# Two RMS norms of a second transformer block applied behind their projections instead of ahead of them, and the spread of a rate row moved behind the third query tile

## The chip, the cores and the metric

The kernel runs on one core of a Trainium2 chip. TensorE (PE) multiplies matrices into PSUM, VectorE (DVE) and ScalarE (ACT) work element by element, GpSimd (POOL) does one elementwise job here and issues a few DMAs, and SyncE (SP) issues nearly all DMAs. The metric is the time of one execution in microseconds (us); lower is better.

## The reference, cut to what matters

Two blocks run one after the other on a sequence of 512 tokens of width 1024, all in fp32. The first ends with a mixture of experts and a norm; the second begins with a norm of that norm's result, and has another norm ahead of its feed-forward part:

```
# end of the first block
h2 = rmsnorm(x, norm2_w[l])
x = x + expert_choice_ffn(h2, w_router[l], w_gate[l], w_up[l], w_down[l])
...
return rmsnorm(x, norm_f_w)
# second block
h = rms_norm(x, pre_mix_g[l])
proj = h @ w_in[l]          # q, k, v; a recurrent branch; two gates
...
merged = gate_a * (y_a @ proj_a[l]) + gate_b * (y_b @ proj_b[l])
x = x + rms_norm(merged @ w_out[l], post_mix_g[l])
hf = rms_norm(x, pre_ffn_g[l])
u = jnp.square(jax.nn.relu(hf @ w_up[l])) @ w_down[l]
x = x + rms_norm(u, post_ffn_g[l])
```

A norm multiplies each token's row by one number, its rate (one over the root of the mean square), and each column by a weight. The rate of a token is a factor of every product of that token's row with a matrix, so it can be applied to the product as well.

## The kernel before, in words

All work is written out by hand, a queue of instructions per engine, with semaphores between them. The activations lie as `X`, tokens on partitions in 4 tiles (`tc`) of 128, and as `HT`, features on partitions in 8 tiles (`dc`) of 128 by 512 tokens.

Projections take fp32 numbers apart into a high and a low part: ScalarE copies a 1 MB block of weights in rounded form (`split2_act`), GpSimd subtracts that from the block (`splits2_pool`, one instruction per block), and TensorE does three products for each of the 8 `dc` (`split_tile`), 24 matmuls for one tile of 128 output features. Two tiles use one block of weights. Activations are taken apart likewise: ScalarE writes the rounded `HT` (`norm_out_act`), VectorE writes the rest (`norm_low_dve`), for the second block in `LOW3` and `LOW4`. Weight blocks rotate through three slots and two buffers for the high part, so a block is split when the block two before it has been used.

A norm before a projection was done like this. ScalarE squares and sums the rows of `X`, takes a logarithm and an exponential, each of another table, and has the rates `rs`. VectorE makes four diagonal matrices of them (`norm_dve`). TensorE multiplies `X` by the diagonals, which transposes and scales at once (`norm_pe`, 32 matmuls). ScalarE and VectorE then write the high and low parts, and the first projection tile follows them `dc` by `dc`. While TensorE waits for the rates it multiplies something that nobody uses (`keep_busy`).

Where the blocks meet: the last scatter of the experts adds 8 results in PSUM to `ACCX` on VectorE, and each finished row tile is multiplied there by the weight of the first block's last norm, `NORMF`, into `X`. ScalarE squares both (`final1_act`), so that one rate for both norms comes out. The load of the first weight block for the second block (`("qk", 0)`) starts when the last scatter is done.

ScalarE copied the query and key tiles (`band_act`), the 14 tiles of the recurrent branch (`shift_act`) and the relu of the 32 feed-forward tiles (`ffn_act`) out of PSUM, and took the tanh of the gates from PSUM directly (`merge2_act`). Two PSUM banks took turns. GpSimd waited for `n4_dg`, the diagonals of the second norm, before it split the first feed-forward block `("u", 0)`.

The opening of the first block already had its rate behind the projections: `rates_pe` multiplies a matrix of ones by the diagonals, which gives a tile with each token's rate in every row, and `rates_dve` multiplies the cosine and sine tables by it. It stood behind the second query tile, and each tile's rotation (`rotate`) behind the following one.

## Time and profile before

| | |
|---|---|
| median of 3 runs | 2925.87 us (2925.63 to 2927.24) |
| profiled execution | 2916.92 us, span 2915.1 us |
| mean granted TensorE clock | 0.969 of full |
| TensorE busy | 2641.9 us, 91% |
| VectorE busy | 940.4 us, 32% |
| ScalarE busy | 747.0 us, 26% |
| GpSimd busy | 590.8 us, 20% |

The profile is of one execution, and that one was about 9 us shorter than the median of the runs. Differences are therefore worked out inside the profile. TensorE's row says which engine carries the span; where it stands idle, the bracket at the end of its row names how long and what ended the idle time. The end of a pipelined matmul is modelled, so starts are read rather than ends. The places that matter here are three: about 26 us (the opening), 1895 to 1970 us (between the blocks) and 2527 to 2560 us (ahead of the feed-forward part).

### The profile page before, as it was taken

To read this page: it belongs to the slowest core of one execution; us is meant where nothing else is said; L and a number is where in the kernel's file an instruction comes from. 1 tells how busy PE (TensorE), PEld (TensorE's weight loads), DVE (VectorE), ACT (ScalarE), POOL (GpSimd) and SP (SyncE) were. 2 spreads that over 40 slices of the span, in tenths; PEclk is the share of its full clock that TensorE was granted. 3 is DMA by queue.
4 is the path that set the end of the run, shared out by engine and by line. 5 is a ranking of instruction groups with operands and counts; after the bars stand their busy time and mean duration, and the time that the engine had idled before them with its cause. 6 is when DMAs were issued, how large, how long until landed. Compare 5 with 4: busy or idle time off the path is not lost.

```text
span 2915.1 us, 34223 instructions
## 1 busy us (share of the span) xinstructions
PE 2641.9 (91%) x14415; PEld 1726.3 (59%) x14415; DVE 940.4 (32%) x1655; ACT 747.0 (26%) x1258; POOL 590.8 (20%) x181
## 2 busy tenths in 40 slices
PE   8999979889999998898889988898968899999998
PEld 6766767676658542332333323365757766888886
DVE  3267766753212301101011011034474521240221
ACT  3257634532112010010000100054341222422222
POOL 3301645622122000000000000031301022244442
PEclk9999979989999999999999999999988999999999
DMA  4302203113225799999999999942200033322231
GB/s 160 116 16 77 69 30 116 58 40 121 87 84 219 299 428 428 428 428 429 429 428 428 429 429 428 383 134 84 66 1 16 2 120 103 109 94 101 87 102 72
DMA packets 131045, 559.37 MB, mean 192 GB/s; under 512 B 7320, under 2 KB 88672, under 8 KB 103272
## 3 DMA queue, kind: packets, MB, share of 16 engines
q1 hardware_dynamic: 130056, 551.28, 48.0%
q0 software_dynamic: 864, 6.29, 0.6%
q8 instruction: 95, 1.56, 0.2%
q14 instruction: 30, 0.25, 0.0%
HBM read 547.01 MB, written 10.54 MB: 191 GB/s over the span
## 4 chain that ended last, share of the span: by engine, by line
PE 70%; DMA 13%; DVE 9%; ACT 5%; issue 2%; POOL 0%; DVEq 0%; SPq 0%; ACTq 0%; POOLq 0%
DMA S<-in_w_up 11%; PE PS L611 8%; PE PS L613 8%; PE PS L612 8%; PE PS L2211 7%; PE PS L2178 7%; PE PS L601 4%; PE PS L2161 2%; PE PS L3327 2%; PE PS L3330 2%; PE PS L3329 2%; PE PS L3174 2%; PE PS L2222 1%; DMA S<-in_w_down 1%; PE PS L597 1%
## 5 line engine op out<-in xcount | busy, mean ns | idle before, releaser
L2473 POOL TENSOR_TENSOR r_block<-S,r_block 128x2048 fp32r<-128x2048 f32 x57 | 261.5, 4588 | 1484.8 <-ACT r_block L2462 1476.0
L2178 PE MATMUL PS<-S 128*64 128x512 f32 x2048 | 457.1, 596 | 72.9 <-DMA S<-in_w_up 68.7
L611 PE MATMUL PS<-r_block,r_block 128*128 128x512 f32 x1040 | 417.8, 402 | 4.2 <-POOL r_block L2473 2.0
L613 PE MATMUL PS<-r_block,r_block 128*128 128x512 f32 x1040 | 405.3, 390 | 0.0
L612 PE MATMUL PS<-r_block,r_block 128*128 128x512 f32 x1040 | 404.8, 389 | 0.0
L2178 PEld LDWEIGHTS PS<-S 128*64 128x64 f32 x2048 | 141.0, 137 | 379.8 <-issue 247.4
L491 POOL TENSOR_TENSOR r_block<-S,r_block 128x2048 fp32r<-128x2048 f32 x40 | 183.4, 4586 | 550.4 <-ACT r_block L483 330.1
L2211 PE MATMUL PS<-S 128*64 128x512 f32 x1024 | 225.6, 597 | 6.3 <-DMA S<-in_w_down 3.1
L611 PEld LDWEIGHTS PS<-r_block,r_block 128*128 128x128 f32 x1040 | 195.3, 188 | 50.6 <-issue 9.2
L612 PEld LDWEIGHTS PS<-r_block,r_block 128*128 128x128 f32 x1040 | 195.4, 188 | 45.2 <-issue 6.0
L613 PEld LDWEIGHTS PS<-r_block,r_block 128*128 128x128 f32 x1040 | 195.2, 188 | 41.4
L2345 DVE SCALAR_TENSOR_TENSOR S<-S,PS 128x512 f32<-128x512 f32 x32 | 22.0, 687 | 486.9 <-ACT S L2273 463.5
L2211 PEld LDWEIGHTS PS<-S 128*64 128x64 f32 x1024 | 75.8, 138 | 145.1 <-issue 140.4
L2462 ACT ACTIVATE r_block<-S 128x2048 fp32r<-128x2048 f32 x57 | 108.9, 1912 | 172.2 <-PE PS L3330 117.6
L601 PE MATMUL PS<-S 128*128 128x512 f32 x256 | 110.5, 592 | 0.0
L2352 DVE TENSOR_TENSOR S<-S,PS 128x512 f32<-128x512 f32 x32 | 20.6, 684 | 257.2 <-PE PS L2178 257.2
L483 ACT ACTIVATE r_block<-S 128x2048 fp32r<-128x2048 f32 x40 | 76.4, 1909 | 99.6 <-DMA S<-in_w_in 68.8
L3327 PE MATMUL PS<-r_block,r_block 128*128 128x512 f32 x256 | 99.8, 390 | 1.4 <-ACT S L3346 1.4
L3329 PE MATMUL PS<-r_block,r_block 128*128 128x512 f32 x256 | 99.6, 389 | 0.0
L3330 PE MATMUL PS<-r_block,r_block 128*128 128x512 f32 x256 | 99.6, 389 | 0.0
L3369 DVE TENSOR_TENSOR S<-S 128x512 f32<-128x512 f32 x32 | 37.9, 1185 | 188.7 <-ACT S L3346 188.7
L601 PEld LDWEIGHTS PS<-S 128*128 128x128 f32 x256 | 48.6, 190 | 59.6 <-issue 59.3
(478 smaller groups left out, 3702.4 us busy)
## 6 DMA issues: line engine op xcount, KB each, us to landing
S<-in_w_gate SPq DMA_DIRECT2D x64, 2048.0 KB, 18.0
S<-in_w_up SPq DMA_DIRECT2D x64, 2048.0 KB, 21.0
S<-in_w_down SPq DMA_DIRECT2D x64, 2048.0 KB, 25.6
S<-in_w_in SPq DMA_DIRECT2D x57, 1024.0 KB, 5.4
S<-in_w_up SPq DMA_DIRECT2D x16, 1024.0 KB, 5.4
S<-in_w_down SPq DMA_DIRECT2D x16, 1024.0 KB, 4.8
S<-decay_rows SPq DMA_DIRECT2D x8, 1024.0 KB, 6.9
S<-in_w_out SPq DMA_DIRECT2D x8, 1024.0 KB, 5.0
```

Of the source, the lines that this page charges most:

```text
L491: pool.tensor_tensor(r32(w), w, rounded(WH[k % 2]), ALU.subtract).then_inc(sem("w_low"), 1)
L601: mm = pe.matmul(out, w[:, dc, off:off + P], src[:, dc, :], start=(dc == 0), stop=(dc == DC - 1))
L611: pe.matmul(out, wh, r32(HT[:, dc, :]), start=(dc == 0), stop=False)
L612: pe.matmul(out, wh, r32(low[:, dc, :]), start=False, stop=False)
L613: mm = pe.matmul(out, wl, r32(HT[:, dc, :]), start=False, stop=(dc == DC - 1))
L2178: mm = pe.matmul(PS[c * CAP:(c + 1) * CAP, 2 + 2 * m + g, :], XE[:, 2 * q + r, e * CAP:(e + 1) * CAP], w[:, r, 1024 * g + 512 * c:1024 * g ...
L2211: mm = pe.matmul(PS[c * CAP:(c + 1) * CAP, 6 + half, :], HE[e][:, f, :], w[:, f % 4, 512 * half:512 * half + 512], start=(f == 0), stop=(f ...
L2462: act.activation(r32(WH[k % 2]), slot2(name), ACT.Copy).then_inc(sem("w2_high"), 1)
L2473: pool.tensor_tensor(r32(w), w, rounded(WH[k % 2]), ALU.subtract).then_inc(sem("w2_low"), 1)
L3327: pe.matmul(PS[:, n, :], uh, r32(grid(wh.rearrange("p a b -> p (a b)"), 2)[:, f % 2, s]), start=first, stop=False)
L3329: pe.matmul(PS[:, n, :], uh, r32(wl[:, f % 2, s]), start=False, stop=False)
L3330: mm = pe.matmul(PS[:, n, :], ul, r32(grid(wh.rearrange("p a b -> p (a b)"), 2)[:, f % 2, s]), start=False, stop=last)
```

## The change

The opening uses four banks (0, 1, 5, 6) and four buffers for the raw query and key tiles, rates stand behind the third tile, and rotations one tile later. In the second block both norms are applied behind their projections. Unscaled `X` is transposed as its row tiles get ready, the high and low parts are made at once, and the rates are worked out while the first three tiles run. A tile `RSB` with the rates in every row is then spread (`spread_rates_pe` behind the third tile, `spread_rates_dve`), and VectorE multiplies each projection by it on its way out of PSUM. The weight of the first block's last norm goes into `pre_mix` for the projections, and into `X` by `block1_rows_dve`.

```diff
@@ attention_pe, opening
-                split_tile(pe, PS[:, p % 2, :], parts_of(("qk", p // 2)), P * (p % 2), HTL, "n1_lo" if p == 0 else None)\
-                    .then_inc(sem("qk_proj"), 1)
-                if p == 1:
-                    rates_pe(pe)
-                if p:
+                split_tile(pe, PS[:, QK_BANK[p % 4], :], parts_of(("qk", p // 2)), P * (p % 2), HTL, "n1_lo" if p == 0 else None)\
+                    .then_inc(sem("qk_proj"), 1)
+                if p == 2:
+                    rates_pe(pe)
+                    rotate(0)
+                if p >= 2:
                     rotate(p - 1)
@@ experts_pe, new: the last scatter, with the transposes between
+            def last_scatter():
+                pe.wait_ge(*count("mo_y", 4 * PAIRS))
+                for m in range(8):
+                    if m >= 2:
+                        pe.wait_ge(*count("mo_acc", 8 * (PAIRS - 1) + m - 1))
+                    pe.matmul(PS[:, 6 + m % 2, :], (SELT, SELT2)[m % 2][:, (m // 2) * P:(m // 2 + 1) * P],
+                              YE[:, 512 * (m % 2):512 * (m % 2) + 512], start=True, stop=True)\
+                        .then_inc(sem("mo_scattered"), 1)
+                    if m % 2 and m >= 3:
+                        first_turns(m // 2 - 1)
+                first_turns(TC - 1)
+                pe.wait_ge(*count("mo_acc", 8 * PAIRS))
+                for dc in (6, 7):
+                    for tc in range(TC):
+                        mm = pe.transpose(PS[:, dc, block_of(tc)], X[:, tc, block_of(dc)], ident)
+                    mm.then_inc(sem("n3_tp"), 1)
@@ experts_dve
-                dve.tensor_tensor(x, x, PS[:, m % 2, :], ALU.add).then_inc(sem("mo_acc"), 1)
-                if m % 2:
-                    dve.wait_ge(*count("mo_acc", 8 * (PAIRS - 1) + m + 1))
-                    dve.tensor_tensor(X[:, m // 2, :], ACCX[:, m // 2, :], NORMF, ALU.mult).then_inc(sem("x2_done"), 1)
+                dve.tensor_tensor(X[:, m // 2, s], ACCX[:, m // 2, s], PS[:, 6 + m % 2, :], ALU.add).then_inc(sem("mo_acc"), 1)
+                if m in (3, 5):
+                    weighted_rows_dve(dve, m // 2 - 1)
@@ new
+        def weighted_rows_dve(dve, tc):
+            dve.wait_ge(*count("mo_acc", 8 * (PAIRS - 1) + 2 * (tc + 1)))
+            if tc >= 2:
+                dve.wait_ge(*count("n3_sq", tc))
+            dve.tensor_tensor(XW[tc], X[:, tc, :], NORMF, ALU.mult).then_inc(sem("n3_w"), 1)
+        def block1_rows_dve(dve):
+            dve.wait_ge(*count("f1_r", 1))
+            for tc in range(TC):
+                dve.scalar_tensor_tensor(X[:, tc, :], X[:, tc, :], rs1[:, tc:tc + 1], NORMF, ALU.mult, ALU.mult)\
+                    .then_inc(sem("x2_done"), 1)
+        def spread_rates_pe(pe, tag, low):
+            pe.wait_ge(*count(tag + "_dg", TC))
+            pe.wait_ge(*count(low, DC))
+            for tc in range(TC):
+                mm = pe.matmul(PS[:, 4, block_of(tc)], ones, diag[:, tc, :], start=True, stop=True)
+            mm.then_inc(sem(tag + "_rates"), 1)
@@ splits2_pool
-                    if name == ("u", 0):
-                        pool.wait_ge(*count("n4_dg", TC))
@@ query and key tiles of the second block, now on VectorE
-                act.activation(dst, PS[:, p % 2, :], ACT.Copy).then_inc(sem("b_qk_done"), 1)
+                dve.tensor_tensor(dst, PS[:, p % 4, :], RSB, ALU.mult).then_inc(sem("b_qk_done"), 1)
@@ recurrent branch, now on VectorE
-                act.activation(PADR[:, t % 2, 1:1 + T], PS[:, t % 2, :], ACT.Copy).then_inc(sem("r_copied"), 1)
+                dve.tensor_tensor(pad[:, 1:1 + T], PS[:, t % 2, :], RSB, ALU.mult).then_inc(sem("r_copied"), 1)
@@ gates
-                        act.activation(MG_T[:, 2 * (m - 2) + j, :], PS[:, 2 * m + j, :], ACT.Tanh, scale=0.5,
-                                       bias=s_gbh[:, g:g + 1]).then_inc(sem("m2_tanh"), 1)
+                        act.activation(gate, gate, ACT.Tanh, scale=0.5, bias=s_gbh[:, g:g + 1]).then_inc(sem("m2_tanh"), 1)
+                        dve.tensor_tensor(MG_T[:, 2 * m + j, :], PS[:, 4 + 2 * m + j, :], RSB, ALU.mult).then_inc(sem("m2_scaled"), 1)
@@ ffn_pe
-            keep_busy(pe, 0, 20)
-            pe.wait_ge(*count("pn1_x", TC))
-            norm_pe(pe, "n4")
+            keep_busy(pe, 0, 12)
+            pe.wait_ge(*count("o2_copied", 8))
+            for tc in range(TC):
+                pe.wait_ge(*count("pn1_x", tc + 1))
+                for dc in range(DC):
+                    mm = pe.transpose(PS[:, dc, block_of(tc)], X[:, tc, block_of(dc)], ident)
...
-                    if t == FH * hf and hf:
-                        pe.wait_ge(*count("dn_part", 2))
-                    if t >= 2:
-                        pe.wait_ge(*count("up_relu", t - 1))
+                    if hf and t < FH + 4:
+                        pe.wait_ge(*count("dn_part", t - FH + 1))
+                    if t >= 4:
+                        pe.wait_ge(*count("up_relu", t - 3))
@@ feed-forward relu, now on VectorE
-                    act.activation(RL[:, t % 2, :], PS[:, t % 2, :], ACT.Relu).then_inc(sem("up_relu"), 1)
+                dve.scalar_tensor_tensor(r, PS[:, t % 4, :], 0.0, RSB, ALU.max, ALU.mult).then_inc(sem("up_relu"), 1)
@@ block2_pe and block2_sp
-            pe.wait_ge(*count("x2_done", TC))
-            keep_busy(pe, 7, 10)
-            norm_pe(pe, "n3")
-                if n == 0:
-                    sp.wait_ge(*count(last_scatter[0], last_scatter[1]))
```

First place: TensorE from the last expert down projection to the first projection tile of the second block. L2222 is the last scatter, L597 `keep_busy`, L589 `norm_pe`, L611 to L613 `split_tile`. Before:

```order
L2211 MATMUL PS<-S 64x512 x32
L2222 MATMUL PS<-S 128x512 x8
L597 MATMUL PS<-S 128x256 x10
L589 MATMUL PS<-S 128x128 x32
L611 MATMUL PS<-r_block_584,r_block_582 128x512
L612 MATMUL PS<-r_block_398,r_block_582 128x512
```

Of the change (L2215 is the down projection, L2235 the last scatter, L2251 `first_turns`, L2245 the transposes of the last two feature tiles):

```order
L2215 MATMUL PS<-S 64x512 x32
L2235 MATMUL PS<-S 128x512 x4
L2251 MATMUL PS<-S 128x128 x6
L2235 MATMUL PS<-S 128x512 x2
L2251 MATMUL PS<-S 128x128 x6
L2235 MATMUL PS<-S 128x512 x2
L2251 MATMUL PS<-S 128x128 x12
L2245 MATMUL PS<-S 128x128 x8
L611 MATMUL PS<-r_block_583,r_block_581 128x512
```

The 10 unused products and the 32 scaling ones are gone, and 32 transposes stand in and behind the scatter.

Second place: ScalarE over the same stretch. L2385 and L2387 are squares, L2462 is `split2_act`, L566 `norm_out_act`, L2389 to L2395 the logarithms and exponentials. Before:

```order
L2385 ACTIVATE S<-S 128x1024
L2387 ACTIVATE S<-S 128x1024
L2389 ACTIVATE S<-S 128x4
L2391 ACTIVATE S<-S 128x4
L2393 ACT_TABLE_LOAD
L2393 ACTIVATE S<-S 128x4
L2395 ACTIVATE S<-S 128x4
L2462 ACTIVATE r_block_582<-S 128x2048
L566 ACTIVATE r_block_584<-PS,S 128x512 x4
L566 ACTIVATE r_block_601<-PS,S 128x512 x4
L2401 ACTIVATE S<-S 128x1024 x4
L2462 ACTIVATE r_block_651<-S 128x2048
```

Of the change (L2418 and L2423 are the squares, L2524 the split, from the first square on):

```order
L2418 ACTIVATE S<-S 128x1024
L2524 ACTIVATE r_block_581<-S 128x2048
L2423 ACTIVATE S<-S 128x1024
L2418 ACTIVATE S<-S 128x1024
L2423 ACTIVATE S<-S 128x1024
L566 ACTIVATE r_block_583<-PS,S 128x512 x4
L566 ACTIVATE r_block_600<-PS,S 128x512 x4
L2524 ACTIVATE r_block_641<-S 128x2048
L2418 ACTIVATE S<-S 128x1024
L2423 ACTIVATE S<-S 128x1024
L2418 ACTIVATE S<-S 128x1024
L2423 ACTIVATE S<-S 128x1024
```

The first split stands behind one square instead of all eight, the high parts behind four, and the rates come last.

Third place: ScalarE ahead of the feed-forward part, from the exponential of the norm behind the mixing part (L3280) on. L507 to L519 are `norm_act`, L3346 the relu. Before:

```order
L3280 ACT_TABLE_LOAD
L3280 ACTIVATE S<-S 128x4
L507 ACT_TABLE_LOAD
L507 ACTIVATE S<-S 128x1
L514 ACTIVATE S<-S 128x1024 x4
L517 ACTIVATE S<-S 128x4
L519 ACT_TABLE_LOAD
L519 ACTIVATE S<-S 128x4
L2462 ACTIVATE r_block_651<-S 128x2048
L566 ACTIVATE r_block_584<-PS,S 128x512 x4
L566 ACTIVATE r_block_601<-PS,S 128x512 x4
L2462 ACTIVATE r_block_582<-S 128x2048
```

Of the change (L3349 is that exponential, L2524 the split):

```order
L3349 ACT_TABLE_LOAD
L3349 ACTIVATE S<-S 128x4
L2524 ACTIVATE r_block_641<-S 128x2048
L566 ACTIVATE r_block_583<-PS,S 128x512 x4
L566 ACTIVATE r_block_600<-PS,S 128x512 x4
L2524 ACTIVATE r_block_581<-S 128x2048
L3417 ACT_TABLE_LOAD
L3417 ACTIVATE S<-S 128x1
```

Squares and rates now stand behind the high parts and behind the second split.

## Rows read from the trace of the kernel before

**Rows 1.** The page's first part: busy time of the engines.

```profile
PE 2641.9 (91%) x14415; PEld 1726.3 (59%) x14415; DVE 940.4 (32%) x1655; ACT 747.0 (26%) x1258; POOL 590.8 (20%) x181
```

**Rows 2.** TensorE between the blocks: start, duration, line, tile, count, idle before and releaser.

```profile
1895.91 3.96 PE L2222 MATMUL PS<-S 128*128 128x512 f32 x8 [1.39 <-ACT S L2288]
...
1907.26 4.58 PE L597 MATMUL PS<-S 128*128 128x256 f32 x20 [2.33 <-DVE S L2373]
1911.68 7.31 PE L589 MATMUL PS<-S 128*128 128x128 f32 x64
1918.74 0.47 PE L611 MATMUL PS<-r_block,r_block 128*128 128x512 f32 x1
...
1930.39 0.50 PE L611 MATMUL PS<-r_block,r_block 128*128 128x512 f32 x1 [0.50 <-POOL r_block L2473]
```

**Rows 3.** VectorE between the blocks, same view.

```profile
1898.62 1.23 DVE L2373 TENSOR_TENSOR S<-S 128x1024 f32<-128x1024 f32 x1
...
1904.67 1.28 DVE L2370 TENSOR_TENSOR S<-S,PS 128x512 f32<-128x512 f32 x2
...
1913.49 7.01 DVE L577 SCALAR_TENSOR_TENSOR r_block<-PS,S,r_block 128x512 fp32r<-128x512 f32 x8 [2.08 <-ACT r_block L566]
```

**Rows 4.** ScalarE between the blocks, same view.

```profile
1898.62 1.06 ACT L2385 ACTIVATE S<-S 128x1024 f32<-128x1024 f32 x1 [1.34 <-DVE S L2370]
...
1910.55 1.91 ACT L2462 ACTIVATE r_block<-S 128x2048 fp32r<-128x2048 f32 x1
```

**Rows 5.** DMA issues between the blocks (KB each, us to landing), and SP's queue.

```profile
S<-in_w_in SPq DMA_DIRECT2D x13, 1024.0 KB, 5.4
...
1905.02 1.02 SPq L3487 DMA_DIRECT2D S<-in_w_in  x2
```

**Rows 6.** TensorE and ScalarE in the opening.

```profile
7.86 5.90 PE L545 MATMUL PS<-S 128*128 128x128 f32 x32 [7.86 <-DMA S<-in_x]
26.67 1.16 PE L553 MATMUL PS<-S 128*128 128x128 f32 x8 [0.75 <-DVE S L571]
...
13.10 4.73 ACT L566 ACTIVATE r_block<-PS,S 128x512 fp32r<-128x512 f32 x8 [4.92 <-PE PS L545]
```

**Rows 7.** TensorE, ScalarE and VectorE ahead of the feed-forward part.

```profile
2527.66 8.79 PE L597 MATMUL PS<-S 128*128 128x256 f32 x40
2540.48 9.01 PE L589 MATMUL PS<-S 128*128 128x128 f32 x64 [4.03 <-DVE S L571]
2549.25 0.47 PE L611 MATMUL PS<-r_block,r_block 128*128 128x512 f32 x1
...
2531.28 0.21 ACT L3280 ACTIVATE S<-S 128x4 f32<-128x4 f32 x1
...
2531.52 4.87 DVE L3286 SCALAR_TENSOR_TENSOR S<-S 128x1024 f32<-128x1024 f32 x4 [0.63 <-ACT S L3280]
```

**Rows 8.** VectorE and GpSimd where GpSimd splits a block of weights.

```profile
2065.57 0.75 DVE L2760 SCALAR_TENSOR_TENSOR S<-S 128x512 f32<-128x512 f32 x1
2066.24 5.11 DVE L2758 TENSOR_TENSOR S<-S 128x512 f32<-128x512 f32 x1
...
2066.09 4.71 POOL L2473 TENSOR_TENSOR r_block<-S,r_block 128x2048 fp32r<-128x2048 f32 x1 [1.10 <-ACT r_block L2462]
...
668.90 2.35 DVE L1736 SCALAR_TENSOR_TENSOR S<-S 128x512 f32<-128x512 f32 x1
...
666.10 4.61 POOL L491 TENSOR_TENSOR r_block<-S,r_block 128x2048 fp32r<-128x2048 f32 x1 [7.98 <-ACT r_block L483]
```

**Rows 9.** Busy time by window: PEclk is the third value from the end.

```profile
2542.00:2544.00 2.00, 2.00 (x12) 2.00 (x11) 0.86 (x2) 1.02 (x2) 2.00 (x1) 0.50 0.05 12
```

**Rows 10.** The feed-forward part: a relu, a square, and TensorE's start of the second half.

```profile
2571.33 0.60 ACT L3346 ACTIVATE S<-PS 128x512 f32<-128x512 f32 x1 [4.84 <-PE PS L613]
...
2566.52 1.56 DVE L3369 TENSOR_TENSOR S<-S 128x512 f32<-128x512 f32 x1 [3.56 <-ACT S L3346]
...
2725.82 0.47 PE L611 MATMUL PS<-r_block,r_block 128*128 128x512 f32 x1 [1.22 <-issue]
```

More of the change, by code:

```diff
@@ L642, in build_program @@
         A0 = M_DYN + 20480
-        qk_raw = at(A0, 2, T)
+        qk_raw = [at(A0 + o, T) for o in (0, 512, 2048, 2560)]
+        QK_BANK = (0, 1, 5, 6)
         qk_tmp = at(A0 + 1024, 2, T)
@@ L669, in rotate @@
                     pe.wait_ge(*count("qk_sin", p - 1))
-                pe.matmul(PS[:, 2 + p % 2, :], const("rot"), qk_raw[:, p % 2, :], start=True, stop=True)\
+                pe.matmul(PS[:, 2 + p % 2, :], const("rot"), qk_raw[p % 4], start=True, stop=True)\
                     .then_inc(sem("qk_rot"), 1)
@@ L2256, in experts_pe @@
             pe.wait_ge(*count("mo_he", 4 * PAIRS))
-            scatter(PAIRS - 1)
+            last_scatter()
         def experts_act(act):
@@ L2388, in final1_act @@
+            act.activation(warm, eps, ACT.Ln).then_inc(sem("f1_ln"), 1)
+            squares(0)
+            squares(1)
+            act.wait_ge(*count("both_norms", 1))
+            norm_out_act(act, "n3", "pre_mix")
+            split2_act(act, ("qk", 1))
+            squares(2)
+            squares(3)
             act.wait_ge(*count("f1_sq", TC))
```

146 lines of the change are left out of this document (90 added, 56 removed), and 2 rows, old and new, of the table CHAINS.

## The prediction

> **What bounds the kernel.** I read the busy times first: TensorE is busy 91% of the span and no other engine over 32% [rows 1], so time is won where TensorE stands idle or does work that nobody uses. The expert stage in the middle is paced by its weight stream and is not edited. Then I read TensorE's timeline at the three edited places. Between the blocks the last scatter runs from 1895.91 to about 1904.9, unused products fill from 1907.26, the scaling products run from 1911.68, and the first projection tile starts at 1918.74 [rows 2]. That is 13.8 us without a projection. Ahead of the feed-forward part the unused products start at 2527.66, the scaling ones at 2540.48 after 4.03 us idle, and the first tile at 2549.25: 21.6 us [rows 7]. In the opening TensorE waits 0.75 us for the diagonals [rows 6].
>
> **The opening.** Behind the third tile the diagonals are long there, so the 0.75 us go. The rate and rotation products stay the same in number. Four banks and buffers remove waits that the timeline does not show as stalls; I take nothing for them. Saved: 0.75 us.
>
> **Between the blocks.** A scatter product takes 3.96 / 4 = 0.99 us [rows 2], an addition on VectorE 1.28 / 2 = 0.64 and a multiplication of 1024 columns 1.23 [rows 3], a transpose 5.90 / 32 = 0.18 at most [rows 6]. TensorE now does 4 scatters (to 1899.9), 6 transposes, 2 scatters, 6 transposes, 2 scatters, 6 transposes, and is at about 1906.6. VectorE adds the fourth result by 1900.7, weights row tile 0 by 1902.0, adds the sixth result by 1903.7 and then comes to weighting row tile 1.
>
> Here a lock matters. While GpSimd splits a block (4.6 us), VectorE instructions with two inputs in SBUF stand still: one square of 512 columns took 5.11 us, from 2066.24 to 2071.35, where the split ran from 2066.09 to 2070.80, and the three-operand kind took 2.35 us for 0.75 beside a split that ended at 670.71 [rows 8]. VectorE had been working without a gap there, and GpSimd, which was ready at 2066.09, still came in at VectorE's next instruction. When will GpSimd split here? The load of the first block no longer waits for the last scatter, so it is issued at 1894.6 instead of 1905.02 and lands after 5.4 us [rows 5], at 1900.0. ScalarE finishes its first square of 1.06 us plus the reading of its sum at 1899.8 and splits until 1902.0, in 1.91 us [rows 4]. GpSimd then holds the lock from 1902.1 to 1906.7. Row tile 1 is weighted only at 1907.9, and the last two additions, which are queued behind it, end at 1909.2. The last transposes wait for those. ScalarE's first high part (0.69) and VectorE's first low part (0.7) follow, and the first projection tile starts at 1910.9. Before it was 1918.74: 7.8 us saved.
>
> The high parts come every 4.73 / 8 = 0.59 us [rows 6] and a tile takes 0.60 + 4.84 = 5.44 us, 0.68 per `dc` [rows 10], so the first tile is not slowed much. The second block's split follows the high parts: ScalarE until 1916.1, GpSimd until 1921.4, needed at 1910.9 + 10.9 = 1921.8, so the 0.50 us that TensorE waited at 1930.39 [rows 2] go too. The rates: two more pairs of squares, one weighting that waits for that split, two logarithms, a table and an exponential put the diagonals at 1927.0; the third tile ends at 1927.3. They are just hidden. Spreading them adds one set of rate products, 1.16 us in the opening [rows 6]; 1.1 us of TensorE. Sum: 7.8 + 0.5 - 1.1 = 7.2 us saved.
>
> **Query, recurrent and gate tiles.** VectorE multiplies by `RSB` where ScalarE copied: 0.64 against about 0.5 us, with one SBUF input, so the lock doesn't hold it: the eight low parts, with the same kinds of inputs, ran at TensorE's pace beside a split (7.01 us, from 1913.49 on, ScalarE's split having ended at 1912.5 [rows 3, 4]). Per tile of 5.44 us VectorE has two or three more instructions, of which one may stand behind a split of 4.6 us. A bank must be free two tiles later, which leaves over 3 us. Cost 0. The four row tiles of the first block's norm, 4 x 1.23 us, stand in VectorE's queue behind the third tile; four banks cover them. The last gate now passes VectorE and then ScalarE, about 0.85 us later. Behind it stand a product, two sums, two roundings and two subtractions of 0.4 to 0.7 us each, and the split of the second output block, 4.6 us, which is needed 10.9 us after the gate tile. That was some 9.7 us and becomes 10.6. Cost 0, or 0.3 if that is short.
>
> **Ahead of the feed-forward part.** ScalarE's exponential ends at 2531.49 and VectorE starts the four row tiles of the residual at 2531.52, 4.87 / 4 = 1.22 us each [rows 7]. Before, ScalarE then squared, and GpSimd waited for the diagonals. Now ScalarE splits at once, until 2533.4, and GpSimd wants the lock in the middle of the second row tile. It gets it at 2533.96, and holds it until 2538.6. Row tiles 2 and 3 then end at 2539.8 and 2541.0. These are three-operand instructions with two SBUF inputs, the kind that stood still [rows 8]. The last transposes, the first high and low part: the first feed-forward tile starts at 2542.8, not 2549.25. Saved 6.4 us.
>
> The Trainium skill (SBUF — State Buffer, "SBUF: two separate sides") says that whichever of the two starts first has the shared pair for its whole instruction and the other fully blocks. It does not say who is next when VectorE has a row of instructions. Were it VectorE, GpSimd would split from 2536.4 to 2541.0, and the tile would start at 2541.1, 1.7 us sooner; the row at 2066.24 says GpSimd.
>
> From this: TensorE is idle from about 2535.3 to 2539.9. Before, it was idle 4.03 us, and then the granted clock was at its lower level, 1.2 of 2.4 GHz, in the window 2542 to 2544 [rows 9]. I expect the same stretch to fall on the first tile, whose `dc` then take up to 1.36 us instead of 0.68; over some 2.3 us of it that is 1.2 or 1.3 us lost (the scaling products lost as much before, 9.01 against 7.31 us [rows 2, 7], but ahead of the tile and inside the 6.4). The rate products cost 1.1 again. At the start of the second half TensorE waited 1.22 us for two copies of ScalarE [rows 10] and now waits for one: 0.5 saved. Sum: 6.4 - 1.3 - 1.1 + 0.5 = 4.5 us saved.
>
> **VectorE in the feed-forward tiles.** Per two tiles it does 2 x 4 instructions (relu, square, rounding, subtraction) of 0.69 us at most, 5.5 us, and one split may block it for 4.6. That is 10.1 of 10.88 us. The square beside a split took 1.56 us [rows 10]. It starts three tiles late, behind the spread rates, and TensorE waits only for the relu of four tiles back, so the lag is worked off. Cost 0 in my sum.
>
> **The sum.** 0.75 + 7.2 + 4.5 = 12.4 us of the profiled execution, 2916.9 to 2904.5. Its own time is 9 us below the median of the runs; the difference carries over: 2925.9 - 12.4 = 2913.5 us. Unknown prices: the lock at both starts (0 to 4.6 and 0 to 2.1 us more saved if VectorE is not held, and 1.2 for the clock with it), the clock between the blocks (0 or 1.2 lost), the rates coming late (0 to 2 lost at each start), the last gate (0 to 0.3).
>
> **Rivals.**
> A, the lock costs less: GpSimd comes later than I think, or VectorE keeps its row. Then the first tiles start at 1908.8 and 2538.2 to 2541.1, and 16 to 20 us are saved: 2906 to 2910. For it: the margins at 1902 and 2533 hang on single microseconds. Against: the row at 2066.24.
> B, half is given back: the diagonals are ready 0.3 us before they are needed, the second split 0.4 us, both behind queues that I added up. If each slips by 1 to 2 us at both places, and the clock falls at both, 5 to 8 us go and 5 to 7 remain: 2919 to 2921. What speaks against it: ahead of the feed-forward part the rates have 1.6 us and the second split 0.9 us to spare.
> C, slower: VectorE becomes the bound of the feed-forward tiles. It decides once VectorE's work and the split together exceed 10.88 us per two tiles; they are 10.1. To end 0.2% above before, the 12.4 us and 5.9 more must be lost over 16 pairs, 1.15 us each, so 12.0 us per pair: the relu from PSUM times a tile in SBUF would have to take 1.6 us, not 0.69. Additions with the same operands took 0.64 [rows 3]. Price then 2932 or more.
>
> **Numbers.** The forecast 60%, A 17%, B 17%, C and the like 6%. 0.2% is 5.9 us, about what a measurement of this kernel can tell from no change. All of the forecast and A and over half of B save more: faster 0.86, same 0.09, slower 0.05. Range 2906 to 2921.
>
> **What would show it.** In the profile after: the first tile of the second block at 1910 to 1912 on the old clock of the span (less 0.75), with one VectorE multiplication of 1024 columns that takes 3 to 4 us just before; no idle TensorE behind the first three tiles; the residual's row tiles at 1.2, 1.2, 5.9, 1.2 us and the first feed-forward tile 15.2 us behind the last output product; the lower clock in that tile; relus on VectorE and no wait of TensorE for them until the end of a half. The forecast is wrong if TensorE waits for VectorE in the tiles, or if the two starts come less than 4 us sooner each.

## The result, and the profile after

The changed kernel takes 2907.08 us in the median of 4 runs (2903.94 to 2910.46), the kernel before beside it 2925.75. The ratio is 0.9939, 95% interval 0.9922 to 0.9957: 17.8 us less, with an interval of 12.6 to 22.8. The prediction was 2913.5, in a range of 2906 to 2921. Direction and mechanism hold, and the time lies inside the range, but the 12.4 us of the sum are not what came: the edited places gave 10.5 us by the traces, 2 less than summed, and some 7 us more came from elsewhere, most likely from a place that was not edited. The profiled execution of after took 2910.46 us (span 2908.7).

TensorE of the changed kernel between the blocks, in the columns of [rows 2]:

```profile
1899.41 3.96 PE L2235 MATMUL PS<-S 128*128 128x512 f32 x8 [1.39 <-ACT S L2317]
...
1907.95 0.82 PE L2251 MATMUL PS<-S 128*128 128x128 f32 x6
1912.28 1.54 PE L2251 MATMUL PS<-S 128*128 128x128 f32 x6 [3.51 <-DVE S L2399]
1913.61 1.91 PE L2245 MATMUL PS<-S 128*128 128x128 f32 x8
1915.18 0.78 PE L611 MATMUL PS<-r_block,r_block 128*128 128x512 f32 x1
...
1933.10 1.06 PE L2462 MATMUL PS<-S 128*128 128x128 f32 x8
```

ScalarE's copy of the last down product (L2317, before L2288), which releases the scatter, ends 3.50 us later on this span's clock, at 1899.27 instead of 1895.77; times "behind the down product" are counted from there. From there to the first tile of the second block it is now 15.91 us and was 22.97: 7.06 saved. TensorE's only wait between the scatter's start and that tile is the 3.51 us for VectorE's last additions. VectorE and GpSimd in the same stretch, and VectorE's diagonals:

```profile
1905.14 1.32 DVE L2399 TENSOR_TENSOR S<-S,PS 128x512 f32<-128x512 f32 x2
1906.38 4.64 DVE L2411 TENSOR_TENSOR S<-S 128x1024 f32<-128x1024 f32 x1
1910.95 1.27 DVE L2399 TENSOR_TENSOR S<-S,PS 128x512 f32<-128x512 f32 x2
1913.57 5.36 DVE L577 SCALAR_TENSOR_TENSOR r_block<-PS,S,r_block 128x512 fp32r<-128x512 f32 x8 [1.35 <-ACT r_block L566]
1918.85 1.21 DVE L2411 TENSOR_TENSOR S<-S 128x1024 f32<-128x1024 f32 x1
1921.77 3.85 DVE L2411 TENSOR_TENSOR S<-S 128x1024 f32<-128x1024 f32 x1 [1.71 <-ACT S L2423]
...
1928.96 0.88 DVE L571 TENSOR_SCALAR S<-S 128x128 f32<-128x128 f32 x4 [1.89 <-ACT S L2438]
```

```profile
1905.41 4.53 POOL L2533 TENSOR_TENSOR r_block<-S,r_block 128x2048 fp32r<-128x2048 f32 x1 [980.14 <-ACT r_block L2524]
1919.47 5.07 POOL L2533 TENSOR_TENSOR r_block<-S,r_block 128x2048 fp32r<-128x2048 f32 x1 [9.52 <-ACT r_block L2524]
```

The weighting of row tile 1 takes 4.64 us and not 1.21. The split began a microsecond before it and ends at 1905.41 + 4.53 = 1909.94; the weighting ends 1.08 us later, about its own length. The low parts (L577) run without a pause between the first two splits. The diagonals are done at 1929.84, the rates are used at 1933.10: 3.3 us to spare.

Ahead of the feed-forward part, TensorE, then VectorE, GpSimd and TensorE's granted clock (third value from the end), to be read against [rows 7, 9]:

```profile
2525.69 5.35 PE L597 MATMUL PS<-S 128*128 128x256 f32 x24
2530.98 2.19 PE L3375 MATMUL PS<-S 128*128 128x128 f32 x16
2537.53 3.67 PE L3375 MATMUL PS<-S 128*128 128x128 f32 x16 [4.35 <-DVE S L3355]
2541.36 0.76 PE L611 MATMUL PS<-r_block,r_block 128*128 128x512 f32 x1 [0.16 <-DVE r_block L577]
...
2719.22 0.47 PE L611 MATMUL PS<-r_block,r_block 128*128 128x512 f32 x1 [0.73 <-issue]
```

```profile
2529.55 9.12 DVE L3355 SCALAR_TENSOR_TENSOR S<-S 128x1024 f32<-128x1024 f32 x4 [0.62 <-ACT S L3349]
```

```profile
2531.39 5.00 POOL L2533 TENSOR_TENSOR r_block<-S,r_block 128x2048 fp32r<-128x2048 f32 x1 [20.61 <-ACT r_block L2524]
```

```profile
2539.00:2541.00 2.00, 2.00 (x11) 1.80 (x9) 0.54 (x1) 1.25 (x3) 0.00 (x0) 0.50 0.00 0
2541.00:2543.00 2.00, 1.84 (x5) 1.38 (x5) 2.00 (x4) 2.00 (x5) 0.00 (x0) 0.50 0.00 0
2543.00:2545.00 2.00, 2.00 (x10) 1.63 (x10) 2.00 (x4) 2.00 (x4) 0.00 (x0) 1.00 0.00 0
```

From the unused products to the first tile it is 15.67 us and was 21.59: 5.9 saved. The four residual rows take 9.12 us instead of 4.87. The windows 2529.6:2530, 2533:2534 and 2538:2538.5 show them singly, 1.28, 5.52 and 1.27 us for the first, third and fourth; the second starts at 2530.75 and takes 1.28. The third:

```profile
2531.95 5.52 DVE L3355 SCALAR_TENSOR_TENSOR S<-S 128x1024 f32<-128x1024 f32 x1
```

It was queued behind the second without a gap, and stood still until the split's end at 2536.39. TensorE idles 4.35 us there, and the first tile starts at the lower level, 1.2 of 2.4 GHz; the rise comes at 2543.

To find the rest, I cut the span at the same points of both programs and compared lengths:

| stretch (us) | before | after | difference |
|---|---|---|---|
| last down product to first tile | 22.97 | 15.91 | -7.06 |
| first tile to the first attention scores | 73.98 | 75.69 | +1.71 |
| scores to the product with the LoRA's second factor (L2708, now L2775) | 144.35 | 146.07 | +1.72 |
| that product to the first merge tile: the recurrent branch | 196.48 | 194.67 | -1.81 |
| unused products to first feed-forward tile | 21.59 | 15.67 | -5.92 |
| 16 tiles of the first half | 88.01 | 89.78 | +1.77 |
| down products, to the first tile of the second half | 88.56 | 88.08 | -0.48 |

The stretches left out hardly differ, but for the longest: up to the copy that releases the scatter the changed kernel took 3.50 us more. The spans of this pair differ by 6.4 us only (2915.1 and 2908.7), so this pair can't explain 17.8 us; that is left to the experiments below.

Two other lengths help from here on. The last scatter starts at 1890.5 to 1901.9 us in the fourteen profiles of this case, with a mean of 1897.4 both in the eight with the new opening and in the six with the old one. So that part spreads by 11 us from one execution to the next, and the edit doesn't show in it. From the scatter's start to the end of the span it is 1019.2 us in the profile of before and 1009.3 in that of after.

### The profile page after: what moved, and what is told of

It is laid out like the page before. It is cut to its first block, busy times and chain, and to the rows that moved or that the text cites. A ratio compares the mean times of both kernels' runs of the same rounds, so it can differ in the third digit from the quotient of the medians.

```text
span 2908.7 us, 34078 instructions
## 1 busy us (share of the span) xinstructions
PE 2641.5 (91%) x14331; PEld 1724.0 (59%) x14331; DVE 1011.0 (35%) x1732; ACT 713.6 (25%) x1200; POOL 597.7 (21%) x181
## 4 chain that ended last, share of the span: by engine, by line
PE 71%; DMA 13%; DVE 9%; ACT 4%; issue 2%; POOL 0%; DVEq 0%; SPq 0%; ACTq 0%; POOLq 0%
DMA S<-in_w_up 11%; PE PS L611 8%; PE PS L613 8%; PE PS L612 8%; PE PS L2215 7%; PE PS L2182 7%; PE PS L601 4%; PE PS L2165 2%; PE PS L3403 2%; PE PS L3406 2%; PE PS L3405 2%; PE PS L3241 2%; PE PS L2226 1%; DMA S<-in_w_down 1%; DVE PS L1205 1%
## 5 line engine op out<-in xcount | busy, mean ns | idle before, releaser
L2533 POOL TENSOR_TENSOR r_block<-S,r_block 128x2048 fp32r<-128x2048 f32 x57 | 268.5, 4710 | 1467.8 <-ACT r_block L2524 1459.0
L611 PE MATMUL PS<-r_block,r_block 128*128 128x512 f32 x1040 | 418.5, 402 | 3.2 <-POOL r_block L2533 1.5
L613 PE MATMUL PS<-r_block,r_block 128*128 128x512 f32 x1040 | 406.0, 390 | 0.0
L491 POOL TENSOR_TENSOR r_block<-S,r_block 128x2048 fp32r<-128x2048 f32 x40 | 183.3, 4583 | 552.1 <-ACT r_block L483 329.5
L2215 PE MATMUL PS<-S 128*64 128x512 f32 x1024 | 225.6, 597 | 6.0 <-DMA S<-in_w_down 2.7
L611 PEld LDWEIGHTS PS<-r_block,r_block 128*128 128x128 f32 x1040 | 195.9, 188 | 49.4 <-issue 8.8
L613 PEld LDWEIGHTS PS<-r_block,r_block 128*128 128x128 f32 x1040 | 195.6, 188 | 41.6
L2524 ACT ACTIVATE r_block<-S 128x2048 fp32r<-128x2048 f32 x57 | 109.2, 1918 | 366.3 <-PE PS L613 195.2
L2215 PEld LDWEIGHTS PS<-S 128*64 128x64 f32 x1024 | 75.8, 138 | 144.7 <-issue 140.0
L1405 DVE SCALAR_TENSOR_TENSOR PS<-S,PS 128x512 f32<-128x512 f32 x96 | 72.4, 755 | 6.9 <-ACT PS L1345 4.3
```

Source lines behind the costliest of these rows:

```text
L491: pool.tensor_tensor(r32(w), w, rounded(WH[k % 2]), ALU.subtract).then_inc(sem("w_low"), 1)
L611: pe.matmul(out, wh, r32(HT[:, dc, :]), start=(dc == 0), stop=False)
L613: mm = pe.matmul(out, wl, r32(HT[:, dc, :]), start=False, stop=(dc == DC - 1))
L2215: mm = pe.matmul(PS[c * CAP:(c + 1) * CAP, 6 + half, :], HE[e][:, f, :], w[:, f % 4, 512 * half:512 * half + 512], start=(f == 0), stop=(f ...
L2524: act.activation(r32(WH[k % 2]), slot2(name), ACT.Copy).then_inc(sem("w2_high"), 1)
L2533: pool.tensor_tensor(r32(w), w, rounded(WH[k % 2]), ALU.subtract).then_inc(sem("w2_low"), 1)
```

## The experiments

Every kernel was timed against the kernel before on the same chip. Stretches are named as in the table.

**The changed kernel again, and its three parts.** One part each of the change: the opening, the stretch between the blocks with the tiles behind it, the start of the feed-forward part with its relus. Of each the lines that name it:

```diff
# opening alone
-                if p == 1:
+                if p == 2:
                     rates_pe(pe)
# between the blocks alone
+                    if m % 2 and m >= 3:
+                        first_turns(m // 2 - 1)
# feed-forward part alone
-            norm_pe(pe, "n4")
+                    if t == 2:
+                        spread_rates_pe(pe, "n4", "n4_lo")
```

> The kernel before with the opening alone changed (rates behind the third tile, four banks and buffers). Theory (the three places add up as read from the trace): 0.9 us faster than before, a ratio near 0.9997, which a timing can't tell from 1; in the trace no idle TensorE ahead of the rate products, and a lead of 0.9 us at the end of the query and key tiles. Rival (the opening brings more than its own stall, because what follows falls into other phases): 3 to 5 us faster.

> The kernel before with only the norm between the blocks moved behind its projections (query, recurrent and gate tiles on VectorE too), without the opening and the feed-forward part. Theory: 7 to 8 us faster, the first tile of the second block some 15 us behind the start of the last scatter instead of 22.8, and nothing given back or gained in the recurrent branch and the gates. Rival (the moved copies help or hurt as well): 11 us or more, or under 5.

> The kernel before with only the norm ahead of the feed-forward part moved behind its projection, with four banks and the relu on VectorE, and without GpSimd's wait for the diagonals. Theory: 4.5 to 5 us faster: the first feed-forward tile 15.7 us behind the last output product instead of 21.6, less 1.1 us of rate products and with 0.5 us at the half's start. Rival (VectorE, which is behind in the first tiles, costs TensorE time): under 3 us.

> The changed kernel again, on the same chip as its parts. Theory: the sum of the parts, 13 us; the 18 us measured first would then hold 5 us that belong to differences from one execution to the next, outside the edited places. Rival: 18 us again, and the parts don't add up.

Measured, each beside a median of 2925.39 us before:

| kernel | median us | ratio, 95% interval | its stretch in the trace |
|---|---|---|---|
| opening | 2923.72 | 0.9993 [0.9983, 1.0002] | the 0.75 us wait is gone |
| between | 2912.80 | 0.9957 [0.9940, 0.9974] | 15.89 us to the first tile |
| feed-forward | 2921.91 | 0.9989 [0.9975, 1.0002] | 15.68 us to the first tile |
| all three | 2908.78 | 0.9944 [0.9927, 0.9962] | both |

The parts add up: 1.7 + 12.6 + 3.5 = 17.8 us, all three 16.6. Opening and feed-forward part are, within their intervals, what their stretches show. The part between the blocks gives 12.6 us where its own stretch gives 7.1, less 0.5 behind it; the 7 to 8 us expected of it lie at the edge of its interval (7.6 to 17.6), and the number is that of its rival, 11 or more. The 13 us expected of all three lie inside the interval (11 to 21) and below the number; the parts do add up. The traces show the other 6 us in the recurrent branch: in the two kernels whose second block is there that of before it took 202.13 and 202.28 us, in the three that have the new stretch 193.01 to 194.67. The code of the branch is the same but for its copies, and the copies are not the cause: a kernel below has the old ones and 194.80 us.

**Where the recurrent branch loses 8 us.** TensorE in its first inverse, the opening-alone kernel first, then the kernel before in another execution:

```profile
2218.40 1.05 PE L597 MATMUL PS<-S 128*128 128x256 f32 x2
2219.38 1.88 PE L1085 MATMUL PS<-S 32*32 32x16 f32 x122
2222.92 0.30 PE L1085 MATMUL PS<-S 32*32 32x16 f32 x6 [1.66 <-issue]
2223.14 3.78 PE L597 MATMUL PS<-S 128*128 128x256 f32 x8
```

```profile
2211.99 0.98 PE L597 MATMUL PS<-S 128*128 128x256 f32 x2
2212.93 1.91 PE L1083 MATMUL PS<-S 32*32 32x16 f32 x128
2214.77 3.78 PE L597 MATMUL PS<-S 128*128 128x256 f32 x8
```

In the first, TensorE stops after product 122 of a run of 128 and waits 1.66 us for nothing that the profile names ("issue"). These products take 1.9 us / 128 = 15 ns each. The only transfer near it is one packet of the instruction queue. Its place, in 40 slices of 0.05 us (windows 2219 to 2221 and 2211 to 2213):

```profile
GB/s 0 0 0 0 0 0 0 0 0 0 0 0 0 0 0 0 0 0 0 0 0 0 0 0 0 328 0 0 0 0 0 0 0 0 0 0 0 0 0 0
q8 instruction: 1, 0.02, 3.7%
```

```profile
GB/s 0 0 0 0 0 0 0 0 0 0 0 0 0 0 0 0 0 0 0 0 328 0 0 0 0 0 0 0 0 0 0 0 0 0 0 0 0 0 0 0
q8 instruction: 1, 0.02, 2.9%
```

With the stop the packet comes at 2220.25, 0.9 us behind the start of the run; without it at 2212.00, 0.9 us ahead of it. The same reading of every such run (there is one in each of the two inverses; minus is ahead of its start):

| kernel | first run: packet, stop (us) | second run: packet, stop (us) |
|---|---|---|
| before | -0.43, none | +1.01, 2.14 |
| before, another execution | -0.91, none | -0.94, none |
| opening alone | +0.91, 1.66 | +1.05, 2.21 |
| feed-forward part alone | +1.41, 2.00 | +0.96, 2.14 |
| six instructions fewer (below) | +1.00, none | +1.04, none |
| six more in before (below) | -1.15, none | -1.07, none |
| the eight with the new stretch between the blocks | +1.04 to +1.65, none | +0.99 to +1.48, none |

With the old code ahead of the branch, all five stops have a late packet and the three runs without a stop an early one. With other code a late packet goes without a stop, so it is not enough by itself. And the clock (third value from the end), the opening-alone kernel, then before's other execution:

```profile
2224.00:2228.00 4.00, 4.00 (x50) 2.90 (x50) 1.24 (x3) 0.00 (x0) 0.00 (x0) 0.50 0.02 4
2228.00:2232.00 4.00, 4.00 (x82) 3.11 (x78) 0.00 (x0) 3.06 (x5) 0.00 (x0) 0.50 0.00 2
2232.00:2236.00 4.00, 4.00 (x38) 2.93 (x35) 2.07 (x3) 1.88 (x3) 0.00 (x0) 0.54 0.01 4
```

```profile
2217.00:2221.00 4.00, 3.98 (x72) 2.67 (x70) 0.33 (x1) 1.00 (x2) 0.00 (x0) 0.74 0.00 0
2221.00:2225.00 4.00, 3.69 (x87) 3.14 (x88) 2.07 (x3) 3.85 (x7) 0.00 (x0) 1.00 0.02 6
```

Both have the lower level when the run starts; TensorE had waited for VectorE in the small steps before, 0.98 us the last time. Without the stop the upper level is back 6 us behind the run's start (2219.1), with it 16 us behind (2235.7). A stop of 1.7 or 2.0 us, the lower level for 10 us more, and a second stop of 2.1 or 2.2 us in the other inverse are together of the size of the 7.5 us between 194.7 and 202.2. The profile of before, with the second stop alone, has 196.48: 1.8 us are the second's and the other 5.7, up to 202.2, are the first's with the clock behind it. Is the stop bound to a place in the program, or to chance?

**The kernel before once more.**

> The kernel before, unchanged, profiled once more. The stretch from the product with the LoRA's second factor (tiles of block 2) to the first merge tile took 196.5 us in the profile of before, and 202.1 and 202.3 us in the two experiments whose code there is the same; 193.0 to 194.7 us in the three kernels with the change between the blocks. Theory I (issue): TensorE's sequencer stands still for 2 us at fixed places of the program, and in before's program one or two of these fall into the chain of 32x32 products of the inverse. Then this profile has the stall of 2.1 us at the last 32x32 products again (it was there in all three), and perhaps the one of 1.7 to 2.0 us in the first inverse, which two of three had; the stretch is 202 us with both, 196.5 with one. Theory II (chance): the stalls come and go with the execution; then this profile may have neither, and the stretch is 194.

2915.18 us, the branch 194.71 us, and no stop over 1 us in it: the second theory, for this execution. It was a short one, though: 12 us under the median of 2927.08 of before's runs on that chip, so it says little about most of them. In four profiles of this code between the blocks (before, opening alone, feed-forward alone, this one) the branch took 196.48 with one stop, 202.13 and 202.28 with two, 194.71 with none.

**Six TensorE instructions fewer ahead of it.** 10 unused products of 256 columns become 4 of 512.

```diff
-            keep_busy(pe, 7, 10)
+            keep_busy(pe, 7, 4, 512)
```

> The kernel before with the filler products between the blocks as 4 of 512 columns instead of 10 of 256: six TensorE instructions fewer ahead of the recurrent branch, as in the changed kernel, at about the same busy time, and nothing else. Theory I (issue, by place in the program): the stall moves out of the last 32x32 products; the stretch of the recurrent branch falls from 202 to 194 us, no stall over 1 us is left in the inverse, and the time is 5 to 8 us under before (ratio 0.9975). Theory II (chance): same as before, ratio 1.000, stalls as in before. Theory III (what saves it is another thing of the change between the blocks, such as the later rate or the third slot's time): same as before.

2918.00 us against 2927.08, ratio 0.9960 [0.9945, 0.9974]: 9.1 us less, for an edit that removes no time from the stretch it is in (23.70 us to the first tile, against 22.97). The branch took 194.80 us, without a stop, as the first theory says, and this in the longest of its six executions (2923.31). The packets came 1.0 us behind the runs' starts all the same. That the place where TensorE has nothing left to issue moved behind the 128 products would fit, but no trace shows it.

**Six more in the changed kernel.**

```diff
+                    if m == 2:
+                        keep_busy(pe, 5, 6, 16)
```

> The changed kernel with six filler products of 16 columns behind the second product of the last scatter, where TensorE waits for the accumulation: six instructions more ahead of the recurrent branch, as many as before has, for at most 0.5 us. Theory I (issue): the stall of 2.1 us is back in the last 32x32 products of the inverse, the stretch goes from 194 to 196 to 202 us, and the kernel is 3 to 8 us slower than the changed one (2911 to 2916 us). Theory II and III: 2908 us, no stall over 1 us in the inverse.

2907.35 us, ratio 0.9919 [0.9901, 0.9936]; branch 194.43 us, no stop. The stop did not come back, so the first theory missed. The number of matmuls alone does not set the place: around the first run the packets come +68, +77 and +82 us behind the LoRA product in the changed kernel, +75, +78 and +84 in before's other execution. Six products more or fewer move these by 2 us at most.

**Six more in the kernel before.**

```diff
-            keep_busy(pe, 7, 10)
+            keep_busy(pe, 7, 16, 160)
```

> The counterpart of the kernel with six fewer: the kernel before with the filler between the blocks as 16 products of 160 columns instead of 10 of 256, six TensorE instructions more at the same busy time. Found by now: in two profiles of before's code TensorE stood still for 1.7 and 2.0 us behind product 121 or 122 of the 128 products of 32x16 of the first inverse, a packet of the instruction queue having come only 1.2 us before, and the clock then stayed at its lower level for 8 us more; with six instructions fewer the end of the supply falls behind those 128 products, into filler products. Theory I (place): six more put it at product 115 or 116, still inside them; the stall stays, in the profile with about seven chances in ten, and the median is that of before within 0.1% (2925 to 2928 us). Theory II (any other code than before's loses the stall, or the six fewer won by something else that a changed filler does): 2918 us as with six fewer, and no stall.

2921.39 us against 2925.43, ratio 0.9988 [0.9979, 0.9998]: 4.0 us less, between both expectations. Its profile has no stop; the branch took 194.87 us. But that execution, 2915.60 us, was the shortest of its twelve, so its lack of a stop doesn't stand for the others. The first theory is not carried in its strict form. What stands: stops in 3 of 4 profiles of the code as before ahead of the branch, in none of 10 of other code there, and with the old code a late packet at each stop. What makes the packet late, why it does no harm with other code, and why six more helped at all, stays open.

**Can the split be kept away from VectorE?** Between the blocks, row tile 1 is weighted behind the low parts, and its second square comes behind the high parts.

```diff
-                if m in (3, 5):
-                    weighted_rows_dve(dve, m // 2 - 1)
+                if m == 3:
+                    weighted_rows_dve(dve, 0)
...
@@ final1_dve
+            weighted_rows_dve(dve, 1)
             weighted_rows_dve(dve, 2)
@@ final1_act
             split2_act(act, ("qk", 1))
+            second(1)
```

Left out are the buffers of the weighted rows and one semaphore count that go with it.

> The changed kernel with the weighting of the second token tile, and its second square on ScalarE, behind the accumulations and the low parts instead of between the sixth and the seventh accumulation. In the changed kernel's profile that weighting took 4.64 us (1906.38) beside GpSimd's split and both last accumulations came behind it. Theory of the shared port: the weighting pays 4.6 us wherever GpSimd splits, and here the path no longer holds it: first tile of block 2 3.5 to 4.6 us sooner after the scatter (11.5 to 12.5 us instead of 15.9); the rate, which had 3.3 us to spare, is just in time or 1 us late; total 3 to 4.5 us under the changed kernel (2904 to 2905 us). Rival: the accumulation, the low parts or the transposes run into the port or ScalarE instead (the split lasts to 1909.9), and less than 1.5 us comes out.

VectorE, then GpSimd, then TensorE:

```profile
1905.89 0.69 DVE L2399 TENSOR_TENSOR S<-S,PS 128x512 f32<-128x512 f32 x1 [0.83 <-PE PS L2235]
1906.75 0.69 DVE L2399 TENSOR_TENSOR S<-S,PS 128x512 f32<-128x512 f32 x1 [0.17 <-PE PS L2235]
...
1916.42 5.42 DVE L2411 TENSOR_TENSOR S<-S 128x1024 f32<-128x1024 f32 x1 [0.15 <-ACT S L2427]
...
1904.14 4.56 POOL L2539 TENSOR_TENSOR r_block<-S,r_block 128x2048 fp32r<-128x2048 f32 x1 [980.16 <-ACT r_block L2530]
1914.54 6.22 POOL L2539 TENSOR_TENSOR r_block<-S,r_block 128x2048 fp32r<-128x2048 f32 x1 [5.84 <-ACT r_block L2530]
...
1898.00 3.96 PE L2235 MATMUL PS<-S 128*128 128x512 f32 x8 [1.39 <-ACT S L2317]
1909.54 0.47 PE L611 MATMUL PS<-r_block,r_block 128*128 128x512 f32 x1 [0.30 <-DVE r_block L577]
```

2904.89 us, ratio 0.9913 [0.9896, 0.9930]. The last additions follow the scatter products at once, beside the split; one of their inputs is in PSUM. To the first tile it is 11.68 us instead of 15.91, as expected: 4.2 saved. A weighting still pays, 5.42 us at 1916.42, where TensorE waits for nothing. Not all of the 4.2 us arrives. The changed kernel itself was not timed on that chip; the one with six small products more took 2907.35 there, 2.5 us longer. The first tile keeps the higher clock and wins 1 us more, but from the attention scores to the LoRA product it is 147.63 us against 146.07, and 147.44 in the kernel with both moves below: 1.4 to 1.6 us given back, for a reason that was not looked for. The Trainium skill (SBUF — State Buffer, "SBUF: two separate sides") has only the shared pair contend, and lists as taking it VectorE's instructions in a two-port mode or with two SBUF inputs; the additions have one input there. The trace agrees, 0.69 us beside the split and 5.42 beside the next.

**The same ahead of the feed-forward part.** ScalarE's split stands ahead of its copies of the second half of the output projection.

```diff
@@ merge2_act
                 if half:
+                    split2_act(act, ("u", 0))
                     act.activation(warm, eps, ACT.Ln).then_inc(sem("pn1_ln"), 1)
@@ ffn_act
-            split2_act(act, ("u", 0))
```

> The changed kernel with ScalarE's split of the first FFN weight tile ahead of its copies of the output projection's second half, instead of behind the first norm's rate; GpSimd's half of that split then runs beside the last output products and is done before VectorE's residual rows. In the changed kernel those four rows took 9.12 us (2529.55) beside GpSimd's split (2531.39, 5.00 us), in the kernel before 4.87 us. Theory of the shared port: the rows take 4.9 us again and the first FFN tile comes 4.0 to 4.5 us sooner after the filler products (11.2 to 11.7 us instead of 15.7); total 4 us under the changed kernel. Rival: the rows pay as much to the next split or to the lower clock of the transposes, or the copies of the output projection come 2 us later for the split ahead of them, and 2 us or less comes out.

> The changed kernel once more, beside the two improved ones. 2907 to 2909 us; in its profile no stall over 1 us in the inverse of block 2, and 193 to 195 us from the LoRA's second product to the first merge tile.

```profile
2520.32 5.35 PE L597 MATMUL PS<-S 128*128 128x256 f32 x24
2525.62 4.59 PE L3376 MATMUL PS<-S 128*128 128x128 f32 x32
2531.10 0.47 PE L611 MATMUL PS<-r_block,r_block 128*128 128x512 f32 x1 [0.89 <-DVE r_block L577]
```

```profile
2524.18 4.87 DVE L3356 SCALAR_TENSOR_TENSOR S<-S 128x1024 f32<-128x1024 f32 x4 [0.63 <-ACT S L3350]
```

```profile
2511.69 4.61 POOL L2533 TENSOR_TENSOR r_block<-S,r_block 128x2048 fp32r<-128x2048 f32 x1 [6.27 <-ACT r_block L2524]
```

```profile
2527.00:2529.00 2.00, 1.90 (x16) 1.44 (x14) 2.00 (x2) 0.00 (x0) 0.00 (x0) 1.00 0.00 0
2529.00:2531.00 2.00, 1.11 (x9) 0.86 (x8) 0.86 (x3) 1.52 (x3) 0.00 (x0) 1.00 0.00 0
```

2899.11 us, the changed kernel beside it 2907.57. The split is over before the rows begin, the rows take 4.87 us again, TensorE stays at 2.4 GHz, and the first tile comes 10.78 us behind the unused products instead of 15.67. The 16 tiles take 88.99 us, so of the 1.77 us above 1.0 is the rate products and 0.8 the clock. The trace gives 4.9 + 0.8 = 5.7 us, where 4 were expected; the medians differ by 8.5, with ranges of 12 and 14 us, and the 2.8 us between are not explained. The changed kernel took what was expected of it, and has no stop in the branch (194.39 us).

**Both.**

> The changed kernel with both: the second weighting behind the low parts, and the first FFN split ahead of the copies. If the two places are independent: 4.2 us (measured in the profile of the first alone, scatter to first tile 11.7 instead of 15.9 us) and 4 us, together 8 us under the changed kernel, 2899 to 2901 us.

2895.69 us, ratio 0.9897 [0.9880, 0.9914]: 11.9 us under the changed kernel in the same comparison, 29.7 under before. Expected were 8 us under the changed kernel, 2899 to 2901 us. In the trace it is 11.68 and 10.78 us at the two starts, and from the scatter's start to the end of the span 999.6 us, against 1007.3 to 1009.3 in three profiles of the changed kernel: 7.7 to 9.7 less. It beats both kernels.

## Why the prediction was right, point by point

- **The opening**, 0.75 us: right. `31.56 1.06 PE L553` has no wait before it, and the first part alone gave 1.7 us, not to be told from 0.7.
- **The first tile between the blocks**, 7.8 us: 7.06. The lock and its order were right: the split began 6.1 us behind the down product (predicted 6.3), it held VectorE's next instruction with two inputs in SBUF, and the last addition ended at 1912.22, 12.95 us behind the down product (predicted 13.4). Mis-sized were the last transposes and the first parts: 2.96 us instead of 1.7. TensorE had idled 3.51 us, and the granted clock was 0.50 from 1913 to 1917, over the transposes and into the first tile.
- **The tiles behind it**, rates 1.1 us and 0.5 won: 0.6 lost by the sum, 1.7 measured. The wait of 0.5 is gone and the rates cost 1.06, so 1.1 is the clock in the first tile, which I had named as unknown (0 or 1.2) and taken at 0. It varies: in five more profiles with the same work there the stretch is 74.45 to 75.44 us where this one has 75.69, a clock price of 0 to 0.9. In the kernel with the later weighting, where TensorE hardly idles and the clock stays up, it is only 0.64 longer than before.
- **Query, recurrent and gate tiles**, 0: right. 146.07 us against 145.67 to 145.95 in five traces with the old code there, so 0.1 to 0.4, of which I count 0.3; the profiled execution of before, with 144.35, was a short one.
- **The feed-forward start**, 6.4 - 1.3 - 1.1 + 0.5 = 4.5: 5.9 - 0.8 - 1.0 + 0.5 = 4.6. Two terms were off by half a microsecond and cancel, which is luck. The 6.4 came out as 5.9: the rows took 9.12 us against the 9.5 forecast (1.28, 1.28, 5.52, 1.27 against 1.2, 1.2, 5.9, 1.2), but from their end to the first tile it took 2.69 us instead of 1.8, with the transposes at the lower clock. And the 1.3 for the clock in the tile came out as 0.8, because the lower level ended at 2543.
- **VectorE in the feed-forward tiles**, 0: right. A rounding took 4.71 us beside a split (2578.70), and TensorE waited for no relu. Rival C is out.
- **Rival A** (the lock costs less): its mechanism is out at both places, 4.64 and 5.52 us for the blocked instructions. Its price was not: 16 to 20 us and 2906 to 2910, and 17.8 us and 2907.08 came. A reader who went by the time alone would take A for shown. Moving the weighting or the split away gave 4.2 and 4.9 us to the first tiles. **Rival B** (rates and second split late): out, 3.3 us to spare where I had 0.3, and TensorE waited for no split there. Its other half, the clock at both starts, came true for 1.1 and 0.8 us.
- **The step that is missing.** The sum was to carry over from the profiled execution to the median. It does not: before's profiled execution had one stop in the recurrent branch and 196.48 us, where the others had 202, and the changed code has none. By the traces of the edited places the change saves 0.75 + 7.1 - 1.7 + 4.6 = 10.8 us, less 0.3 behind the scores, 10.5; measured are 16.6 to 18.7 in three comparisons. With 10.5 the time would have been about 2915, inside the range as well, so it was not the 7 us that put it there. The rest, some 7 us, is the size of the two stops with the clock behind them (7.5 us), and an edit that only shifted the program gave 9.1. That this is where it comes from is supported by the traces; that it happens in nearly every execution of before is inferred from the medians, since only four profiles of that code were taken, and two of them are of short executions. The inference can be put in numbers, as an estimate. The profiled times are some 1.8 us above their spans. Take that and the mean scatter start of 1897.4 us from the medians, and 1026 us are left for before (2925.4), 1008 for the changed kernel (2907.6) and 1019 for the one with six instructions fewer (2918.0). In the traces the same part took 1027.0 us with two stops (opening alone), 1019.2 and 1019.0 in the two of before with one stop and none, 1007.3 to 1009.3 in the changed kernel, 1019.6 with six fewer. So the typical execution of before looks like one with two stops. I read the 9 us between the profiled execution and the median as chance, and did not ask in which stretch it lay; by these numbers some 7 us are the stops and the rest is mostly the part ahead of the scatter.

## What to carry to other kernels

Where two engines share a port, look which of the instructions in front of the critical one have both inputs in SBUF, and move either those or the other engine's long instruction: here the moves brought the first tiles forward by 4.2 and 4.9 us, where the blocked instructions had taken 4.64 and 5.52. Look also at what comes later, since one move lost 1.4 to 1.6 us again in a stretch behind it. Where a profiled execution is shorter than the median by more than the change is worth, cut several profiles of the same code into stretches before trusting a sum made in one. A forecast can land in its range, and a rival's price can be met, for reasons that neither names; only the stretches tell. An edit that takes instructions out can move time in places that it does not touch; a control that shifts the program and nothing else (fewer and wider unused products) costs one run.

## What I had not expected of the hardware

- In a run of 128 products of 15 ns each TensorE stood still for 1.66 to 2.21 us five times, with nothing but "issue" beside it. Each time a packet of the instruction queue came 0.9 to 1.4 us behind the run's start; but in 18 other runs, with other code ahead of them, a packet as late went without a stop. That TensorE had run out of instructions is my reading. Behind the stops in the first inverse, where the clock was at its lower level already, it stayed there 10 us longer.
- A rounding with a single input, in SBUF, was held beside a split as well: 4.71 us at 2578.70 (the split from 2578.05 to 2583.13) where its neighbour took 0.43.
- A norm's rows beside GpSimd's split: 9.12 us for four three-operand instructions, 4.87 us without it. The split came in between two rows that stood in the queue without a gap, as in [rows 8].
- Behind 4.35 us idle 16 transposes took 3.67 us at 1.2 GHz; without an idle time before them 32 took 4.59 at 2.4.
